# Feed-forward up projections of a hybrid diffusion step by seven block products in place of eight, with the sums of blocks on GpSimd

## The reference

```
def conv_ffn(h, w_up, conv_w, conv_b, w_down):      # h 640 x 1024, w_up 1024 x 5632, w_down 2816 x 1024
    u = dwconv(h @ w_up, conv_w, conv_b)            # 3 taps along the tokens, each sequence padded with zeros
    gate, val = jnp.split(u, 2, axis=-1)
    return (jax.nn.silu(gate) * val) @ w_down
```

## Time and profile before

| | |
|---|---|
| median of 3 runs | 2309.95 us (2306.36 to 2314.58) |
| profiled execution: its time, its span | 2307.77 us, 2306.0 us |
| PE busy | 2183.8 us, 95% |
| DVE busy | 1372.4 us, 60% |
| ACT busy | 905.9 us, 39% |
| POOL busy | 186.7 us, 8% |

### The profile page before, as it was taken

One profiled execution on the slowest core, in us unless ns is written; L12 is line 12 of the kernel. 1 busy time (PEld: TensorE's weight loads), 2 busy tenths in 40 slices (PEclk: granted clock), 3 DMA queues, 4 the chain that ended last, 5 costly groups with the idle time before them and its releaser, 6 DMA issues.

```text
span 2306.0 us, 33567 instructions
## 1 busy us (share of the span) xinstructions
PE 2183.8 (95%) x13797; PEld 1906.5 (83%) x13797; DVE 1372.4 (60%) x1959; ACT 905.9 (39%) x1800; POOL 186.7 (8%) x221
## 2 busy tenths in 40 slices
PE   6989989989998899999999999999998999999998
PEld 4868868879877797799999988886556898999997
DVE  4467582365228586675555656787775764655655
ACT  4455472245225563432322323544654531222222
POOL 0000000034006212200000000200000200000002
PEclk8999999999999999999999999999999999999999
DMA  7411206501550121222222222211000122222221
GB/s 312 165 46 53 90 1 223 187 34 69 215 183 10 74 92 57 94 88 65 92 74 64 85 72 64 81 55 42 1 1 14 52 84 79 76 73 74 74 74 46
DMA packets 43702, 192.23 MB, mean 83 GB/s; under 512 B 4992, under 2 KB 4992, under 8 KB 36640
## 3 DMA queue, kind: packets, MB, share of 16 engines
q1 hardware_dynamic: 41328, 176.86, 22.1%
q0 software_dynamic: 2224, 13.24, 1.6%
HBM read 182.47 MB, written 7.60 MB: 82 GB/s over the span
## 4 chain that ended last, share of the span: by engine, by line
PE 61%; DVE 6%; ACT 1%; issue 1%; DMA 0%; POOL 0%; ACTq 0%; DVEq 0%; POOLq 0%
PE pg L1050 31%; PE pg L1089 17%; PE pg L726 2%; PE ps L1298 2%; PE pg L1278 2%; PE ps L898 2%; PE ps L1253 1%; PE pg L1253 1%; PE ps L773 1%; DVE mxs L2421 1%; PE pg L898 1%; PE ps L1109 0%; PE ps L1218 0%; DVE rtb L1891 0%; DVE xlo L1865 0%
## 5 line engine op out<-in xcount | busy, mean ns | idle before, releaser
L1050 PE MATMUL pg<-hh,xhi 128*128 128x320 f32 (+2 forms) x1008 | 313.5, 311 | 9.8 <-DVE hl L1979 9.8
L1050 PE MATMUL pg<-hl,xhi 128*128 128x320 f32 (+2 forms) x1008 | 312.0, 310 | 0.0
L1050 PE MATMUL pg<-hh,xlo 128*128 128x320 f32 (+2 forms) x1008 | 311.9, 309 | 0.0
L1865 DVE TENSOR_TENSOR wlo<-ring,whi 128x1024 fp32r<-128x1024 f32 x127 | 154.6, 1222 | 209.0 <-ACT whi L1343 208.7
L726 PE MATMUL pg<-hh,whi 128*128 128x320 f32 x848 | 207.6, 326 | 10.4 <-DVE wlo L1865 6.3
L1343 ACT CAST whi<-ring 128x1024 fp32r<-128x1024 f32 x127 | 132.2, 1047 | 199.1 <-PE pg L1089 136.4
L1050 PEld LDWEIGHTS pg<-hh,xhi 128*128 128x128 f32 x1008 | 191.9, 190 | 12.1 <-issue 11.9
L1050 PE MATMUL pg<-hh,whi 128*128 128x320 f32 (+1 forms) x640 | 197.7, 309 | 0.0
L1050 PE MATMUL pg<-hh,wlo 128*128 128x320 f32 (+1 forms) x640 | 196.7, 307 | 0.0
L1050 PE MATMUL pg<-hl,whi 128*128 128x320 f32 (+1 forms) x640 | 196.6, 307 | 0.0
L726 PE MATMUL pg<-hl,whi 128*128 128x320 f32 x848 | 195.0, 311 | 0.0
(11 more groups left out here) (349 smaller groups left out, 4684.0 us busy)
## 6 DMA issues: line engine op xcount, KB each, us to landing
ring<-in_wstream SPq DMA_DIRECT2D x229, 512.0 KB, 3.6
adaring<-in_wada SPq DMA_DIRECT2D x21, 1024.0 KB, 4.9
ybuf<-in_wada SPq DMA_DIRECT2D x21, 1024.0 KB, 4.9
adabig<-in_wada SPq DMA_DIRECT2D x6, 1024.0 KB, 17.5
xk<-in_x SPq DMA_DIRECT2D x2, 1280.0 KB, 9.3
yssd_scratch<-ybuf POOLq DMA_DIRECT2D x2, 1280.0 KB, 5.8
xk<-yssd_scratch POOLq DMA_DIRECT2D x1, 2560.0 KB, 9.9
xk<-in_x_tok POOLq DMA_DIRECT2D x1, 2560.0 KB, 10.0
```

The lines of the kernel that those rows point to most:

```text
L1050: last = nc.tensor.matmul(out, w[:, k * P:(k + 1) * P], h[:, k, a:b], start=k == 0 and m == 0, stop=k == KT - 1 and m == 2)
L1865: V.tensor_tensor(lo, flat(ring[:, s % RING]), hi.bitcast(F32), ALU.subtract).then_inc(wlo_ready, 1)
```

## The change

In both layers pairs 0 and 1 stay as they are (they now keep only their own convolution split differently over the engines). For pairs 2 to 21 (20 a layer, 40 in all) the gate tile and the val tile are made together by seven products instead of eight. Features are cut in an upper and a lower half of 4 row tiles each, tokens in even and odd runs of 64 columns (`token_block`), outputs in gate and val. That is a 2 x 2 by 2 x 2 product of blocks, and seven products with combined operands give it. A product is 4 row tiles x 3 = 12 matmuls of 320 columns.

- **Weight sums (POOL, `weight_sums`)**: 4 additions or subtractions of 128 x 512 a pair, in place in the ring. Four units D, E, F, G (8, 8, 4 and 8 row tiles) are then split by ACT and DVE in place of two slots. `E` needs the third sum, `F` the first, `G` the fourth; the third sum overwrites a raw half of D's slot, so it waits until D is split (`UNIT_OF["D", s]`), and the first waits until the F of the pair before is split.
- **Token sums (POOL, `token_sums`)**: 4 subtractions of 128 x 1280 a layer, then a cast (ACT) and a rest (DVE) of each. The first two lie where `xk` (the residual) is, so `xk` goes to DRAM at the start of the stage and comes back in the last group of pairs.
- **Results (DVE, `wino`)**: each product has one of four PSUM banks in turn, and DVE adds the banks together into `wk` and `wsum`: two adds of 320 columns and five pairs of adds of 256 + 64 columns a pair, each with one input in PSUM. ACT copies the first product to `wsum`.
- **Convolution**: the middle tap moves from DVE to ACT (`tap`), the other two stay on DVE (`taps`). The convolution of a pair is done during the next pair.
- **Gating**: the multiplication and `gl` move to POOL (`gate_product`, `gated_rest`), the cast to ACT (`gated_cast`).
- **Gate vector**: `gates` on PE is moved from part 3 to part 4 (after its first token tile) in the feed-forward stages, with ACT's copies of it.

By the plan of the change, D of the next pair is split at place 1 of a pair, E at place 2, F and G at place 3. The core of the diff (order of the queues, without declarations):

```
+            def wino(t):                                    # PE
+                pe.wait_ge(wlo_ready, d + 1)
+                if w: pe.wait_ge(wd_ready, SUMS * w - 3)
+                product(1, d, 0, lambda k: (tokens(hh, k, 0), tokens(hl, k, 0)))
+                pe.wait_ge(wlo_ready, e + 1)
+                pe.wait_ge(tl_ready, 4 * layer + 3)
+                if w: pe.wait_ge(wd_ready, SUMS * w - 2)
+                product(2, e, val, lambda k: (five(t2h[:, k]), five(t2l[:, k])))
+                if w: pe.wait_ge(wd_ready, SUMS * w - 1)
+                product(3, e, 1 - val, ...)
+                pe.wait_ge(wlo_ready, f + 1)
+                if w: pe.wait_ge(wd_ready, SUMS * w)
+                product(4, f, 0, ...)
+                pe.wait_ge(wa_ready, w + 1)
+                product(5, d, 1, ..., tile=True)
+                pe.wait_ge(wlo_ready, g + 1)
+                pe.wait_ge(wd_ready, SUMS * w + 1)
+                pe.wait_ge(tl_ready, 4 * layer + 4)
+                product(6, g, 1 - val, ...)
+                pe.wait_ge(wd_ready, SUMS * w + 2)
+                product(7, g, val, ..., tile=True)
...
+            def wino(t, prev):                              # ACT
+                preps(t)
+                wino_taps(prev)                             # middle taps of gate and val
+                act.wait_ge(wp_ready, PRODUCTS * w + 1)
+                nc.scalar.copy(wsum[:, 0], wino_bank(w, 1)).then_inc(wa_ready, 1)
+                preps(t, 1)
+                gate_silu(prev)
+                preps(t, 2)
+                gated_cast(prev)                            # waits for POOL's gate_product
+                preps(t, 3)
...
+            def wino(t, prev):                              # DVE; sums 1 to 6, the 7th is wino_value
+                wino_value(prev); preps(prev, 3); preps(t)
+                taps(prev)
+                V.tensor_tensor(wsum[:, 1], wino_bank(w, 2), wsum[:, 0], ALU.add).then_inc(wd_ready, 1)
+                preps(t, 1)
+                add_quarter(n, 0, wino_bank(w, 3), wsum[:, 1])[1].then_inc(wd_ready, 1)
+                taps(prev + 1)
+                ...                                         # product 4: wd_ready + 2, product 5: + 1
+                preps(t, 2)
+                add_to_quarter(n, 0, wino_bank(w, 6)).then_inc(wd_ready, 1)
...
+            def weight_sums(t, between=None):               # POOL
+                if w: pool.wait_ge(wlo_ready, UNIT_OF["F", TILES[WINO[w - 1]][2][0][0]] + 1)
+                G.tensor_tensor(s1[:], gate[:, 0:512], gate[:, 512:1024], ALU.add).then_inc(sx_ready, 1)
+                pool.wait_ge(sx_ready, 4 * w + 1)
+                G.tensor_tensor(gate[:, 0:512], val[:, 0:512], gate[:, 0:512], ALU.subtract).then_inc(sx_ready, 1)
+                if between is not None: gated_rest(between)
+                pool.wait_ge(wlo_ready, UNIT_OF["D", s] + 1)
+                G.tensor_tensor(val[:, 0:512], s1[:], val[:, 0:512], ALU.subtract).then_inc(sx_ready, 1)
+                pool.wait_ge(sx_ready, 4 * w + 3)
+                G.tensor_tensor(val[:, 512:1024], val[:, 512:1024], val[:, 0:512], ALU.subtract).then_inc(sx_ready, 1)
...
+            def ffn(layer):                                 # POOL; inside a group of four pairs:
+                weight_sums(t + 2, rest if rest < multiplied else None)
+                gate_product(multiplied)
```

More of the change, by code:

```diff
@@ L141, with units @@
 T_OG = FIRST_OF["og"]
[L144 to L148, removed]
+WINO_FIRST = 2
+WINO = [_t for _t, (_k, _i, _) in enumerate(TILES) if _k == "gate" and _i[1] >= WINO_FIRST]
+WINO_AT = {_t: _w for _w, _t in enumerate(WINO)}
+WINO_LAYER = len(WINO) // 2
+WINO_PARTS = "DEFG"
+WINO_USED = {"D": 5, "E": 3, "F": 4, "G": 7}
+PRODUCTS = SUMS = 7
+def units():
+    out = [("full", s) for s in range(S_LATE)]
+    for t, (kind, i, kts) in enumerate(TILES):
+        if kts[0][0] < S_LATE or t - 1 in WINO_AT or (kind == "mat" and i[2]):
+            continue
+        if t in WINO_AT:
+            out += [(part, kts[0][0]) for part in WINO_PARTS]
+        else:
+            out += [("full", s) for s in sorted({s for s, _, _ in kts})]
+    return out
@@ L1350, in prep, with preps @@
                 prepped[0] = max(prepped[0], upto)
-            def preps(t):
-                for s in PREP_AT.get(t, []):
-                    cast(s)
+            def preps(t, place=0):
+                for u in PREP_AT.get(10 * t + place, []):
+                    cast(u)
             def squares(n, src, waits, width=D_MODEL, tiles=None):
@@ L1638, in up_tile @@
-                conv_in(t, n)
-                if kind == "gate":
-                    act.wait_ge(conv_ready, n + 1)
-                    gi = layer * FFN_T + k
-                    if gi:
-                        act.wait_ge(g_ready, gi)
-                    nc.scalar.activation(sq[:, 0, 0:CP], wk[:, 2 + n % 2, 0:CP], ACT.Silu).then_inc(conv_done, 1)
+                conv_in(t, 12 + 2 * (layer * FFN_T + k) + (kind == "val"))
+                if kind == "gate" and k == 0:
+                    for c in (0, SAMPLE + 1, UP - 1):
+                        last = nc.scalar.copy(wk[:, 0:2, c:c + 1], condT[:, 0:2, 2:3])
+                    link(last)
@@ new lines, in up_tile, with wino_taps @@
+                if kind == "val" and k == WINO_FIRST - 1:
+                    token_sum_cast(layer, 3)
+                act.wait_ge(tile_free[t % 2], t // 2 + 1)
+                tap(t)
+                if kind == "gate":
+                    gate_silu(t)
+                else:
+                    gated_cast(t)
+                    if k == 0:
+                        for i in range(3):
+                            token_sum_cast(layer, i)
+            def wino_taps(t):
+                w = WINO_AT[t]
+                act.wait_ge(wd_ready, SUMS * w + 6)
+                tap(t)
+                act.wait_ge(wd_ready, SUMS * w + 7)
+                tap(t + 1)
@@ L1872, in prep, with preps @@
                 prepped[0] = max(prepped[0], upto)
-            def preps(t):
-                for s in PREP_AT.get(t, []):
-                    rest(s)
+            def preps(t, place=0):
+                for u in PREP_AT.get(10 * t + place, []):
+                    rest(u)
             def ada_bias(r):
@@ L2006, in mat_tile @@
                     return
-                soon = PREP_AT.get(t, [])
-                if tt < TT - 1:
+                soon = PREP_AT.get(10 * t, [])
+                if tt < TT - 1 and not prepped:
                     preps(t)
@@ L2265, in up_tile @@
-                link(last)
-                link(V.tensor_copy(gh[:, gi % G_RING], sq[:, 1, 0:NT]))
-                V.tensor_tensor(gl[:, gi % G_RING], sq[:, 1, 0:NT], gh[:, gi % G_RING].bitcast(F32),
-                                ALU.subtract).then_inc(g_ready, 1)
+                if kind == "val" and k == WINO_FIRST - 1:
+                    token_sum_rest(layer, 3)
+                taps(t)
+                if kind == "val" and k == 0:
+                    for i in range(3):
+                        token_sum_rest(layer, i)
@@ L2270, in stage, with wino_end @@
+            def wino_end(t):
+                wino_value(t)
+                preps(t, 3)
+                preps(t + 2)
+                taps(t)
+                taps(t + 1)
             def stage(name):
```

473 lines of the change are left out of this document (387 added, 86 removed).

## The result

| | before | after |
|---|---|---|
| median | 2310.09 us (2306.36 to 2314.58) | 2360.40 us (2359.94 to 2361.13) |
| runs | 4 | 4 |
| ratio, 95% interval | | 1.0217 (1.0199 to 1.0236) |
| profiled execution: its time, its span | 2307.77, 2306.0 us | 2359.94, 2358.1 us |

The account below looks back on a forecast made before the run. PE was taken to bound the kernel, busy 95% of the span. Layer start, groups, layer end and gate vector sum to -19.9 us a layer, 40 us slower for two: 2350 us against 2310, range 2280 to 2420.

Parts of the forecast that it names:

- start of the layer, to the end of part 0: First changed pair waits for token sums, casts and rests, then PE's clock is lower: 19 us lost a layer.
- groups 2 to 4 with their `mat` parts: Each group of four pairs gains 2.1 us, less 0.5 at the change to the `mat` part: +4.8 a layer.
- group 5: The last group of four pairs in a layer gains 2.1 us before its tail.
- end of the layer: Down projection's fifth k waits 6.0 us more for pair 21; lower clock -2.5, later gate vector -1: -9.5.
- gate vector: In part 3 of the down projection PE no longer waits for this vector: +1.7 us a layer.
- Exclusion: DVE instructions with two SBUF inputs and POOL's SBUF reads take turns: 14.2 us a pair against PE's 12.3.
- The loop: Queue order through POOL, ACT and DVE makes a changed pair take 16.4 us, 2.3 more than before.
- Place in the group: The fourth pair's product 1 starts 41.6 us into a group, which ends at 54.2 in place of 56.3.
- Rival A: PE stays the bound and the kernel gets faster, with a loop under 13.8 us: 2293 us; chance 0.20.
- Rival B: Gains and losses cancel, with a loop of 15 us and layer starts of -12: 2322 us; chance 0.14.
- Rival C: Far slower: loop of 17.3 us each time, PE's clock low at times: 2400 to 2410; 0.24 together with Rival D.
- Rival D: ACT reloads its function table between Identity and Silu, 1.3 us a load, giving Rival C's times; 0.24 together with it.

Follow-up runs that it names:

- experiment 6: Changed kernel with each of POOL's four weight sums replaced by three fills of similar length that read nothing, all waits kept: 2286.25 us, ratio 0.9896.
- experiment 1: Changed kernel with ACT casting F and G of the next pair before the gated cast that waits for POOL's product: 2335.61 us, ratio 1.0125.
- experiments 2: Changed kernel with POOL's four weight sums left out but for 8 columns each, the first a fill with zeros: 2277.83 us, ratio 0.9859.
- experiment 5: Changed kernel with ACT's casts of F and G ahead of the gated cast and seven products only from pair 6 on: 2322.51 us, ratio 1.0053.

## Why the prediction held, step by step

The forecast was 2350 for a measured 2360.4, and the sign, the mechanism and the length of the loop are as it put them; that the loop's length fits to 0.1 us is in part luck, as shown below. By its own terms, for layer 0 (us gained; forecast, then measured):

| term | forecast | measured |
|---|---|---|
| start of the layer, to the end of part 0 | -19 | -18.5 |
| groups 2 to 4 with their `mat` parts | +4.8 | -0.6 |
| group 5 | +2.1 | +1.0 |
| end of the layer | -9.5 | -7.5 |
| gate vector | +1.7 | +1.3 |
| sum | -19.9 | -24.3 |

The measured terms are worked out from the starts of the groups and `mat` parts in both traces, and their sum meets the 24.2 of the stage but for rounding.

- **Exclusion**: as forecast, and now shown by experiment 6. Its price, 14.2 us for a pair, is near the 14.95 of experiment 1, in which DVE has no idle time left. The version with whole durations, 16.3, is over what this loop needed.
- **The loop**: 16.46 for 16.4. It holds one thing that was put aside as the worse bound: E's rest does slip between the two parts of POOL's product, which is recorded as 2.70 us instead of 1.65. A slip was to give 17.3, so other steps of the chain were shorter than put. One is POOL's rest of 640 columns, 1.32 us at its shortest where 1.57 had been read from another line. That such errors meet at 16.46 is luck.
- **Place in the group**: the fourth pair's product 1 at 41.38 for 41.6.
- **Groups 2 to 4**: the step that failed, short by 5.4 us, more than the 4.3 by which the layer as a whole missed. The forecast let a group with its `mat` part gain 1.6 us: 2.1 less 0.5 at the change to the part. Group 3 with its part gains 0.5, and so does group 4 (the time of the gate vector apart), as the wait for the split of the third slot takes up to 2.06 us of the part: 1.1 less, three times. And group 2 loses 2.0 more (55.80 and 53.78 us). Its second product waits 1.74 us for E's rest, because D's slot, which the forecast had split during the part, is cast only at 1124.21 us, 2.5 us before the part ends; E needs the third sum, and that waits for D. ACT, POOL and PE:

```profile
1124.21 1.05 ACT L1515 CAST xhi<-ring 128x1024 fp32r<-128x1024 f32 x1 [21.26 <-PE pg L1199]
1126.60 1.29 POOL L2901 TENSOR_TENSOR ring<-s,ring 128x512 f32<-128x512 f32 x1 [19.63 <-DVE xlo L2129]
1130.39 0.42 PE L1227 MATMUL ps<-t2h,xhi 128*128 128x320 f32 x1 [1.74 <-DVE xlo L2129]
```

  The clock is no third term. The forecast had priced it at the edges of the layer only; in groups 3 and 5 it fell too, and took 1.5 us of the group each time, but behind group 3 the wait in the `mat` part is shorter by the same amount (83.68 us in all, 83.67 where the clock stayed up).
- **Start**: products 1 and 4 of the first changed pair start at 1024.35 and 1040.00; D's rest had been put at 1023.5 and product 4 at 1038.8, and the stage itself starts 1.5 later. The first three token sums, which alternate with DVE's rests, ended at 1007.93 for 1007.4; the shortest of the eight took 2.89 us, their mean with the turns of DVE is 3.52.
- **End**: the gap is 7.07 us in layer 0, the waits of pair 21 as put. In layer 1 it is 9.19: the copy of `xk`, which the forecast had called hidden, holds up a slot there. In layer 0, 2 of the 9.5 us that the trace shows are the gate vector's own time on PE, moved here from part 3.
- **Rival A** (PE stays the bound) needed a loop under 13.8. That is so only without the sums' reading: experiments 2 and 6 give 2278 and 2286, and the forecast had 2281 for a kernel without exclusion. **Rival B** needed a loop of 15 and starts of -12; experiment 1 shows that such a loop (14.95) is there once two casts are moved, but with the start as it is the time was 2336, not 2322. **Rival C** needed 17.3 each time and the clock low at length; the clock fell for a few us in two of the five groups of layer 0, which changed nothing in the sum of group 3 and its part. **Rival D** is refuted by the groups of ACT in the kernel after, between 1017 and 1435 us:

```profile
L1817 ACT ACTIVATE wk<-wk,small 128x641 f32<-128x641 f32 x40 | 35.3, 921 | 2.7 <-DVE wk L2555 1.7 <-DVE wk L2549 1.0
L1828 ACT ACTIVATE sq<-wk 128x641 f32<-128x641 f32 x20 | 14.9, 743 | 44.2 <-DVE wk L2524 44.2
```

40 taps (Identity) alternate with 20 Silus of 743 ns, as long as before, and no row of a table load stands among the groups.

The 3.5 us outside the feed-forward stages lie within what varies there. The rest of the span is 1340.0 to 1346.0 us in nine traces of kernels with the change or an edit of it and 1341.9 in the one of the kernel before, and `ffn0` starts anywhere from 975.7 to 981.7 us. Not settled is how the start of a layer divides between casts, rests and order. It was not tried to have the additions of weights on an engine other than POOL.

## What to carry to other kernels

Work that goes to GpSimd beside a VectorE whose instructions have two SBUF inputs is not parallel work: add the durations of both (less some 0.15 us at each change of hands), and compare the sum with the time of the engine that bounds the kernel, before the arithmetic saved. Then follow one turn of the queues through all engines; moving two casts ahead in ACT's queue gave back 20.6 of the 48.7 us here. Take a group together with what stands behind it: a wait or a low clock in one may only replace a wait in the other. And a fill that takes as long as the operation tells length from exclusion in one run.

## What the runs showed of the hardware that was not expected

- POOL's fills of 512 columns take 0.525 us at the median and leave DVE's taps at 0.88; a subtraction of the same size takes 1.30 alone and turns them to 1.9.
- A POOL subtraction of 1280 columns in runs of 64 takes 2.89 us at the least, 2.25 ns a column; 512 contiguous columns in 1.30 are 2.5, and 640 take 1.32 in one line (2.1) and 1.57 in another. So the runs cost POOL little if anything, and they cost PE nothing (49.25 us for 336 matmuls).
- A DVE cast with a single SBUF input has to wait for POOL as well: three of 30 casts of 512 columns in the kernel before take 1.49 us for 0.42, one of them at 977.82 us beside the POOL instruction of the earlier trace rows.
- The clock fell after two waits of 1.8 and 2.5 us in some groups (0.57 over 4 us) and not in others of the same kernel (1.00), though the waits and the work before them were alike. It changed no sum of a group and its `mat` part (83.7 us).
- A weight slot that stood beside a return of 2.5 MB came late enough to hold ACT for 5.63 us, at 343 GB/s in that stretch (experiment 5), and for 2.66 us in layer 1 of the changed kernel.
